# A transformer program's opening: the second slab's split ahead of the root, rotations at one lag, parameter transposes two units earlier

## The chip, the cores and the metric

One core of one Trainium2 chip. The metric is the device time in microseconds of one execution of the whole program; lower is better.

## The reference, cut to what matters

Two blocks of a network on 256 rows of width 1024, float32. The change lies in the first steps of the first block:

```
n = rms_norm(x, ln_mix_g)
proj = n @ w_in                      # 1024 x 5888
qa, ka, va, ... = split(proj)        # 768 columns each for q, k, v of the dilated attention
qa = rope(qa);  ka = rope(ka)        # 12 heads of 64: x*cos + rot(x)*sin
```

After it come a dilated and a stick-breaking attention, gates, a cross attention with a memory, a convolutional gated MLP, and a second block of two layers, whose last part is a mixture of 8 experts.

## The kernel before, in words

Every float32 product is made of three matmuls on parts: a number is split into a high part (ScalarE copies it to the rounded type) and a residual (VectorE subtracts). The weights come as slabs of 1 MB, transferred on SyncE's queue in the order of a plan into five raw buffers. A slab is split (`begin_split`, line 381: ScalarE's copy at L394 at once, VectorE's residual at L398 when the returned function is called) into one of three split buffers. Slab n goes into buffer n modulo 3, so its split waits until the products of slab n - 3 have released that buffer (`over`), and for the slab's landing. The raw buffer that a residual frees is given to the next transfer (`send`). `W.take` hands slab n to the products and first queues the splits of all slabs up to n + 2 (n + 1 in its first call).

Each engine works through its own queue in the order in which the program appends to it; waits are on semaphores that count an engine's operations.

The opening: x is transposed (`turn_rows`) and split; slab 0 is split in two halves (`split_half`). The squares of x are summed on ScalarE in four pieces (`square_half`, L630); `root_of` (L639 to L511) makes the inverse root from them on VectorE in small steps; `diagonal` (L648) makes two diagonal matrices of it, and `over_columns` (L657, L660) spreads them into R1, with which cosine and sine are multiplied (L786). The normalisation of q and k is thus applied in the rotation.

Then 12 units of 128 columns are made, two to a slab: units 0 to 5 are q, 6 to 11 are k. A unit is 24 matmuls (`wstat`; L438 to L440) into one PSUM bank. `rotate(unit)` multiplies the unit with sine (L769) and with cosine (L770) on VectorE; the second frees the bank. If another rotation is pending, `rope_finish` closes the older one: a pair of matmul records with the matrix `rot` on TensorE (L745) into a new bank, and an add on VectorE (L748). `ps.take()` gives the 8 banks in turn (0 to 7, and round again); each unit, each `rope_finish`, `over_columns` and `other_params` take one.

`other_params` transposes the staged parameters with four matmuls (L709) and copies them to `prm` on ScalarE (L712). They are needed from the memory's rows on. The squares of the memory (`sq2`) are made in the steps of units 5 and 7. Behind unit 11 come the two slabs of v (`v_proj`, "va"); the rotations still open are made after the first of them.

The order of takes up to the loop, from the code: `turn_rows` for k = 0, 1 take banks 0 and 1, the first parameters' transpose 2, `turn_rows` for k = 2 to 7 take 3 to 7 and 0, units 0 and 1 take 1 and 2. In the loop of before: unit 2, `over_columns`, unit 3, unit 4, and from there on finishing pairs and units as the code has them.

Of the kernel before, what the change touches and what calls it, by code (L numbers as in the profile page):

```python
# [154 lines left out]
def program(nc, x, mem, consts, w, out, cap):  # L155
    ctx = ExitStack()
    with ctx:
# [296 lines left out]
        def wstat(W_, o, nH, nL, m, kcs, start, stop, *waits, by=None):  # L454

            H, L, ready, _ = W_

            def product(e, q, a, b):
                return mm3(e, o, H[:, a, m * 128:(m + 1) * 128], L[:, a, m * 128:(m + 1) * 128],
                           nH[:, b, :], nL[:, b, :], start and q == 0, stop and q == len(kcs) - 1)  # L460
            return chunks_of(product, kcs, by, ready, *waits)
# [37 lines left out]
        def newton(cols, t):  # L499


            guess = 1597463007.0 - 2.0 ** 30 - 2.0 ** 22

            def both(make):
                for tb in range(len(cols)):
                    t[tb] = dve.op(make(*cols[tb]), t[tb])
            both(lambda y, d, u: lambda e: e.tensor_scalar(y.bitcast(I32), d.bitcast(I32), -0.5, guess,
                                                           ALU.mult, ALU.add))
            for _ in range(3):
                both(lambda y, d, u: lambda e: e.scalar_tensor_tensor(u, y, y, d, ALU.mult, ALU.mult))  # L510
                both(lambda y, d, u: lambda e: e.scalar_tensor_tensor(y, u, 1.5, y, ALU.add, ALU.mult))  # L511
            return t
# [14 lines left out]
        def stat(q, slot, tb):  # L527
            return sm[:, 32 * q + slot + tb:32 * q + slot + tb + 1]
# [84 lines left out]
        def cload(t, first, last, eng=None):  # L613

            c0, c1_ = CCOL[first][0], sum(CCOL[last])
            return [load(t[:, 0:c1_ - c0], consts[:, c0:c1_], eng=eng)]
# [3 lines left out]
        W = Weights(lambda: lc1.extend(cload(c1, "rot", "sin", sp)))  # L620
# [8 lines left out]
        def square_half(src, junk, slot, tb, h, *waits):  # L629
            return act.op(lambda e: e.activation(  # L630
                junk[:, tb, 512 * h:512 * h + 512], src[:, tb, 512 * h:512 * h + 512], ACT.Square,
                accum_out=stat(3 + h, slot, tb)), *waits)

        def root_of(slot, last):

            t = []
            for tb in range(2):
                c0 = stat(3, slot, tb)
                t.append(dve.op(lambda e, c0=c0: e.tensor_scalar(c0, c0, -0.5 / 1024, -0.5 * EPS, ALU.mult, ALU.add),  # L639
                                last[tb, 0]))  # L640
            for tb in range(2):
                c0, c1_, d = (stat(q, slot, tb) for q in (3, 4, 5))
                t[tb] = dve.op(lambda e, c0=c0, c1_=c1_, d=d: e.scalar_tensor_tensor(
                    d, c1_, -0.5 / 1024, c0, ALU.mult, ALU.add), t[tb], last[tb, 1])
            return sm[:, slot:slot + 2], newton([[stat(q, slot, tb) for q in (0, 5, 6)] for tb in range(2)], t)

        def diagonal(D, r, tr):
            return [dve.op(lambda e, tb=tb: e.tensor_scalar(D[:, tb, :], ident, r[:, tb:tb + 1], None, ALU.mult),  # L648
                           tr[tb]) for tb in range(2)]

        def over_columns(R, D, td, *waits):

            b = ps.take()

            def f(e):
                for tb in range(2):
                    last = e.matmul(banks[b][:, 128 * tb:128 * tb + 128], ones, D[:, tb, :], start=True, stop=True)  # L657
                return last
            t = pe.op(f, td, lc, ps.free[b])
            tR = act.op(lambda e: e.activation(R[:, :], banks[b][:, 0:256], ACT.Copy), t, *waits)  # L660
            ps.free[b] = [tR]
            return tR
# [11 lines left out]
        def split_rows(bt, gname, H, L, k):  # L674
            b, t = bt
            g = split_from_psum(H[:, k, :], L[:, k, :], banks[b][:, 0:256], t, tprm, scale=pcol(gname, k))
            ps.free[b] = g
            return g
# [17 lines left out]
        W.split_half(0)  # L696
        nx += [split_rows(turned[k], "ln_mix_g", nAH, nAL, k) for k in range(4, 8)]
        W.split_half(1)
        sq1[1, 1] = square_half(X, scr, 0, 1, 1, lx[1])
        rx, trx = root_of(0, sq1)  # L700
        tdx = diagonal(D1, rx, trx)
        mem_cols, mem_row = [], []

        def other_params():
            b = ps.take()

            def f(e):
                for i in range(4):
                    last = e.transpose(banks[b][:, i * 128:(i + 1) * 128], stage[:, i, :], ident)  # L709
                return last  # L710
            t = pe.op(f, rest, ps.free[b])
            tp = act.op(lambda e: e.activation(prm[:, 16:512], banks[b][:, 16:512], ACT.Copy), t)  # L712
            ps.free[b] = [tp]
# [28 lines left out]
        def rope_finish():  # L742
            unit, i, tsin, tcos = rope_pending.pop(0)
            b = ps.take()
            t = pe.op(lambda e: e.matmul(banks[b][:, 0:256], rot, rsc[i], start=True, stop=True),  # L745
                      tsin, ps.free[b], lc1)
            dst = (qA if unit < 6 else kA)[:, unit % 6, :]
            t2 = dve.op(lambda e: e.tensor_tensor(dst, banks[b][:, 0:256], rcs[i], ALU.add), t, tcos)  # L748
            rfree[i] = [t, t2]
            ps.free[b] = [t2]  # L750
            qk_ready[unit] = t2
# [11 lines left out]
        def rotate(unit):  # L763

            b, t = made.pop(unit)
            i = rope_n[0] % 2
            rope_n[0] += 1
            wt = [t, trig, rfree[i]]
            t1 = dve.op(lambda e, b=b, i=i: e.tensor_tensor(rsc[i], banks[b][:, 0:256], sinT, ALU.mult), *wt)  # L769
            t2 = dve.op(lambda e, b=b, i=i: e.tensor_tensor(rcs[i], banks[b][:, 0:256], cosT, ALU.mult), *wt)  # L770
            ps.free[b] = [t2]
            rope_pending.append((unit, i, t1, t2))
            if len(rope_pending) > 1:
                rope_finish()

        for unit in range(2, 12):
            if unit % 2 == 0:
                Wt = W.take("qk")
            b = ps.take()
            t = wstat(Wt, banks[b][:, 0:256], nAH, nAL, unit % 2, all8, True, True, ps.free[b], by=nx)  # L780
            if unit % 2:
                W.release(Wt[3], t)
            made[unit] = (b, t)
            if unit == 2:
                tRx = over_columns(R1, D1, tdx)
                trig = [dve.op(lambda e, c=c: e.tensor_tensor(c, c, R1[:, :], ALU.mult), tRx, lc1)  # L786
                        for c in (sinT, cosT)]
            else:
                rotate(unit - 3 + (unit > 4))
                if unit == 4:  # L790
                    rotate(2)
            if unit in (5, 7):
                for h in range(2):
                    sq2[unit // 7, h] = square_half(M, junkM, 2, unit // 7, h, lm)
            if unit == 9:
                other_params()

        def v_proj(key, ncols, dst, nH, nL, ndy):

            bb = [ps.take(), ps.take()]  # L800
            for s in range(2):
                Wt = W.take(key)
                for tb in range(2):
                    t = tstat(Wt, banks[bb[tb]][:, 0:ncols], nH, nL, tb, [(k, 4 * s + k) for k in range(4)],
                              (0, ncols), s == 0, s == 1, ndy, ps.free[bb[tb]] if s == 0 else None)
                    if s == 1:
                        ps.free[bb[tb]] = [dst(tb, banks[bb[tb]][:, 0:ncols], t)]
                W.release(Wt[3], t)
                yield
# [3 lines left out]
        def put(dstf, toks, r, tr):  # L813
            def g(tb, src, t):
                toks.append(act.op(lambda e: e.activation(dstf(tb), src, ACT.Copy, scale=r[:, tb:tb + 1]), t, tr[tb]))
                return toks[-1]
            return g

        nm = []
        for s, _ in enumerate(v_proj("va", 512, put(lambda tb: vA[:, tb, 0:512], va_t, rx, trx), nAH, nAL, nx)):  # L820
            if s == 0:
                for unit in (10, 11):
                    rotate(unit)
                rope_finish()

# [1653 lines left out]
```

How the kernel before makes its waits and increments, by code:

```python
    def wait(self, *waits):  # L90
        need = {}
        for w in flat(waits):
            sem, v = w
            if need.get(sem.name, (None, 0))[1] < v:
                need[sem.name] = w
        for name, (sem, v) in need.items():
            if self.seen.get(name, 0) < v:
                self.seen[name] = v
                self.items.append(lambda e, sem=sem, v=v: e.wait_ge(sem, v))
# [1 line left out]
    def op(self, fn, *waits, inc=True):  # L101
        self.wait(*waits)
        if inc:
            self.n += 1
            self.items.append(lambda e: fn(e).then_inc(self.sem, 1))
        else:
            self.items.append(fn)
        return (self.sem, self.n)
# [95 lines left out]
        def load(dst, src, *waits, eng=None):  # L205
# [1 line left out]
            small_at[0] += 1  # L207
            q = eng or act
            before = (c.sem, c.n)
            t = c.next()
            q.wait(before if before[1] else None, *waits)
            q.items.append(lambda e: e.dma_start(dst, src).then_inc(c.sem, 16))
            return t
# [2190 lines left out]
            def f(e):  # L2404
                with e.If(overflow[q] > 0):
                    for item in inner:
                        item(e)
                with e.Else():
                    if n1 > n0:
                        e.wait_ge(q.sem, n0)
                        e.sem_inc(q.sem, n1 - n0)
                    for count, inc in dmas.items():
                        if count.n > inc:
                            e.wait_ge(count.sem, count.n - inc)
                        e.sem_inc(count.sem, inc)
```

## Time and profile before

| | |
|---|---|
| median of 3 runs | 1889.77 us (1889.28 to 1893.27) |
| the profiled execution | 1892.46 us |
| its span, first to last instruction | 1890.6 us |
| TensorE busy | 97% of the span |
| VectorE, ScalarE busy | 79%, 62% |
| mean granted TensorE clock | 0.993 of full speed |

Times in rows are microseconds from the start of the span. Engines: PE is TensorE, PEld its weight loads, DVE is VectorE, ACT ScalarE, SPq the transfers that SyncE issues. A row of the timeline gives start, duration, engine, line, operation, output and inputs, count, and in brackets the engine's idle time just before and what ended it. Two neighbouring rows may overlap a little, since instructions are pipelined.

### The profile page before, as it was taken

What the parts mean: (1) busy time and instruction counts of PE and PEld (TensorE: products, weight loads), DVE (VectorE), ACT (ScalarE), POOL (GpSimd) and SP (SyncE); (2) the same over time, 40 slices, a digit from 0 to 9 for tenths busy, and PEclk for the clock granted to TensorE, in tenths of its full rate; (3) what the DMA queues carried; (4) which work ended last, traced back from release to release, by engine and by line L of the source; (5) the groups of instructions that cost most, each with busy time, mean ns of one, the idle gap of its engine ahead of it and who ended that gap; (6) DMA issues with size and microseconds to landing.
All of it is one profiled execution on the core that took longest, in us unless ns stands there. A gap on an engine that the chain in (4) does not pass through costs nothing.

```text
span 1890.6 us, 25921 instructions
## 1 busy us (share of the span) xinstructions
PE 1835.4 (97%) x10249; PEld 1594.7 (84%) x10249; DVE 1487.2 (79%) x1633; ACT 1166.1 (62%) x1103; POOL 56.6 (3%) x71
## 2 busy tenths in 40 slices
PE   7999998999999999998999999999999999999997
PEld 7888978899888999996888888888888888888885
DVE  6664667776796655696888889989898898998897
ACT  4445656555553443443777777777777777777775
POOL 0000000000320000230000000000000000000000
PEclk9999999999999999999999999999999999999998
DMA  9434433755461756454799999999999999999993
GB/s 323 139 106 134 157 112 112 244 187 185 132 195 58 227 200 201 124 195 161 269 373 372 361 349 372 360 371 357 350 365 361 375 369 342 365 366 366 371 359 122
DMA packets 258047, 495.70 MB, mean 262 GB/s; under 512 B 9625, under 2 KB 99455, under 8 KB 257919
## 3 DMA queue, kind: packets, MB, share of 16 engines
q1 hardware_dynamic: 253263, 489.04, 73.5%
q10 hardware_dynamic: 4656, 4.93, 0.9%
q8 instruction: 84, 1.38, 0.3%
q14 instruction: 44, 0.36, 0.1%
HBM read 492.89 MB, written 1.05 MB: 261 GB/s over the span
## 4 chain that ended last, share of the span: by engine, by line
PE 89%; DVE 6%; ACT 4%; issue 1%; DMA 0%; DVEq 0%; SPq 0%; ACTq 0%
PE bank L438 27%; PE bank L440 27%; PE bank L439 27%; DVE splitL L398 2%; PE bank L1798 2%; ACT splitH L394 2%; PE bank L2191 1%; PE bank L2122 1%; PE bank L1905 1%; PE bank L1200 0%; PE bank L2161 0%; PE bank L2160 0%; PE bank L899 0%; ACT RAH L480 0%; PE bank L956 0%
## 5 line engine op out<-in xcount | busy, mean ns | idle before, releaser
L398 DVE TENSOR_TENSOR splitL<-raw,splitH 128x2048 fp32r<-128x2048 f32 (+1 forms) x338 | 768.8, 2278 | 170.6 <-ACT splitH L394 163.1
L394 ACT ACTIVATE splitH<-raw 128x2048 fp32r<-128x2048 f32 (+1 forms) x338 | 641.2, 1902 | 151.0 <-PE bank L440 132.8
L438 PE MATMUL bank<-splitH,RBH 128*128 128x512 f32 x960 | 380.9, 397 | 3.4 <-DVE splitL L398 2.4
L440 PE MATMUL bank<-splitH,RBL 128*128 128x512 f32 x960 | 375.1, 391 | 0.0
L439 PE MATMUL bank<-splitL,RBH 128*128 128x512 f32 x960 | 374.7, 390 | 0.0
L438 PE MATMUL bank<-RAH,splitH 128*128 128x256 f32 x1088 | 311.4, 286 | 7.7 <-DVE RAL L484 3.8
L439 PE MATMUL bank<-RAL,splitH 128*128 128x256 f32 x1088 | 307.7, 283 | 0.0
L440 PE MATMUL bank<-RAH,splitL 128*128 128x256 f32 x1088 | 307.7, 283 | 0.0
L438 PEld LDWEIGHTS bank<-RAH,splitH 128*128 128x128 f32 x1088 | 208.4, 192 | 12.0 <-ACT RAH L480 6.6
L438 PEld LDWEIGHTS bank<-splitH,RBH 128*128 128x128 f32 x960 | 180.7, 188 | 40.8 <-ACT splitH L394 2.3
L440 PEld LDWEIGHTS bank<-splitH,RBL 128*128 128x128 f32 x960 | 180.5, 188 | 38.7
L398 DVE TENSOR_TENSOR splitL<-rawx,splitH 128x2048 fp32r<-128x2048 f32 x84 | 192.4, 2291 | 25.4 <-ACT splitH L394 24.1
L439 PEld LDWEIGHTS bank<-splitL,RBH 128*128 128x128 f32 x960 | 181.0, 189 | 35.5
L439 PEld LDWEIGHTS bank<-RAL,splitH 128*128 128x128 f32 x1088 | 208.5, 192 | 1.0
L440 PEld LDWEIGHTS bank<-RAH,splitL 128*128 128x128 f32 x1088 | 208.5, 192 | 0.0
L394 ACT ACTIVATE splitH<-rawx 128x2048 fp32r<-128x2048 f32 x84 | 161.1, 1918 | 46.4 <-PE bank L440 46.4
L438 PE MATMUL bank<-splitH,hTH 128*128 128x512 f32 x448 | 174.5, 390 | 0.0
L439 PE MATMUL bank<-splitL,hTH 128*128 128x512 f32 x448 | 174.4, 389 | 0.0
L440 PE MATMUL bank<-splitH,hTL 128*128 128x512 f32 x448 | 174.3, 389 | 0.0
L398 DVE TENSOR_TENSOR splitL<-rawx_scr,splitH 128x2048 fp32r<-128x2048 f32 x41 | 94.0, 2292 | 11.2 <-ACT splitH L394 10.2
L440 PEld LDWEIGHTS bank<-splitH,hTL 128*128 128x128 f32 x448 | 84.1, 188 | 17.6
L438 PEld LDWEIGHTS bank<-splitH,hTH 128*128 128x128 f32 x448 | 84.1, 188 | 17.1
(324 smaller groups left out, 2245.8 us busy)
## 6 DMA issues: line engine op xcount, KB each, us to landing
raw<-in_moe_wg SPq DMA_DIRECT2D x71, 1024.0 KB, 6.7
raw<-in_moe_wu SPq DMA_DIRECT2D x71, 1024.0 KB, 6.9
raw<-in_moe_wd SPq DMA_DIRECT2D x69, 1024.0 KB, 6.9
rawx<-in_moe_wd SPq DMA_DIRECT2D x29, 1024.0 KB, 7.0
rawx<-in_moe_wu SPq DMA_DIRECT2D x28, 1024.0 KB, 6.8
rawx<-in_moe_wg SPq DMA_DIRECT2D x27, 1024.0 KB, 6.9
raw<-in_w_in SPq DMA_DIRECT2D x24, 1024.0 KB, 6.7
raw<-in_w_up SPq DMA_DIRECT2D x22, 1024.0 KB, 5.1
```

Source lines behind the costliest of these rows:

```text
L394: a = act.op(lambda e: e.activation(h[:, 0:size], r[:, 0:size], ACT.Copy), self.landed[n], over)
L398: d = dve.op(lambda e: e.tensor_tensor(l[:, 0:size], r[:, 0:size], h[:, 0:size].bitcast(F), ALU.subtract), self.landed[n], over, a)
L438: e.matmul(o, lh, rh, start=start, stop=False)
L439: e.matmul(o, lh, rl, start=False, stop=False)
L440: return e.matmul(o, ll, rh, start=False, stop=stop)
L1798: last = e.matmul(banks[b][:, 0:256], diag[:, k, :], hc[:, 0, 2 + k:258 + k], start=(k == 0), stop=(k == 30))
L1905: last = e.matmul(banks[b][:, 0:256], pww[:, k, 128 * u:128 * u + 128], sq[:, k, :], start=(k == 0), stop=(k == 2))
L2122: last = e.matmul(banks[b][:, 256 * c:256 * c + w_], src[:, tb, d:d + 128], Pm[:, tb, 0:w_], start=(tb == 0), stop=(tb == 1))
L2191: last = e.transpose(banks[b][:, 128 * k:128 * k + 128], hh[q % 2][:, 128 * k:128 * k + 128], ident)
```

## The change

Four edits: ScalarE's part of slab 1's split is queued ahead of the last piece of the squares, and its residual ahead of the root; `rotate` is called once in each step from unit 3 on, for the unit three before (before: from unit 5 on for the unit two before, with two calls in the step of unit 4); `other_params` is called in the step of unit 7 instead of 9; the rotation of unit 9 thereby falls behind the first slab of v. The call of `W.take("qk", 1)` further down finds slab 1 split already.

```
         W.split_half(1)
+        rest_of_second = W.begin_split()
         sq1[1, 1] = square_half(X, scr, 0, 1, 1, lx[1])
+        rest_of_second()
         rx, trx = root_of(0, sq1)
         tdx = diagonal(D1, rx, trx)
-        mem_cols, mem_row = [], []
...
             else:
-                rotate(unit - 3 + (unit > 4))
-                if unit == 4:
-                    rotate(2)
+                rotate(unit - 3)
             if unit in (5, 7):
                 for h in range(2):
                     sq2[unit // 7, h] = square_half(M, junkM, 2, unit // 7, h, lm)
-            if unit == 9:
+            if unit == 7:
                 other_params()
...
             if s == 0:
-                for unit in (10, 11):
+                for unit in (9, 10, 11):
                     rotate(unit)
                 rope_finish()
```

## Rows read from the trace of the kernel before

**Rows 1.** The page: busy times by engine, and the chain that ended last.

```profile
PE 1835.4 (97%) x10249; PEld 1594.7 (84%) x10249; DVE 1487.2 (79%) x1633; ACT 1166.1 (62%) x1103; POOL 56.6 (3%) x71
...
PE 89%; DVE 6%; ACT 4%; issue 1%; DMA 0%; DVEq 0%; SPq 0%; ACTq 0%
```

**Rows 2.** Windows: length, busy times with instruction counts, granted clock, DMA share, GB/s.

```profile
26.00:31.00 5.00, 3.49 (x27) 3.06 (x25) 3.13 (x4) 3.08 (x5) 0.00 (x0) 1.00 1.03 407
...
76.00:110.00 34.00, 34.00 (x259) 31.36 (x260) 21.11 (x32) 14.90 (x20) 0.00 (x0) 1.00 0.29 94
```

**Rows 3.** Timeline of TensorE, 17 to 62 us.

```profile
17.77 0.28 PE L440 MATMUL bank<-RAH,splitL 128*128 128x256 f32 x1
19.30 0.35 PE L438 MATMUL bank<-RAH,splitH 128*128 128x256 f32 x1 [1.25 <-DVE splitL L398]
...
28.45 0.60 PE L745 MATMUL bank<-SC,c 128*128 128x256 f32 x2
30.55 0.70 PE L745 MATMUL bank<-SC,c 128*128 128x256 f32 x2 [1.51 <-DVE SC L769]
...
37.26 0.60 PE L745 MATMUL bank<-SC,c 128*128 128x256 f32 x2
...
40.56 0.60 PE L745 MATMUL bank<-SC,c 128*128 128x256 f32 x2
...
47.59 0.60 PE L709 MATMUL bank<-cb,stage 128*128 128x128 f32 x4
...
50.91 0.60 PE L745 MATMUL bank<-SC,c 128*128 128x256 f32 x2
...
60.11 1.02 PE L745 MATMUL bank<-SC,c 128*128 128x256 f32 x4
61.67 0.70 PE L745 MATMUL bank<-SC,c 128*128 128x256 f32 x2 [0.54 <-DVE SC L769]
```

**Rows 4.** Timeline of VectorE, 14 to 61 us.

```profile
14.53 0.21 DVE L639 TENSOR_SCALAR sm<-sm 128x1 f32<-128x1 f32 x2
...
16.87 4.49 DVE L398 TENSOR_TENSOR splitL<-raw,splitH 128x2048 fp32r<-128x2048 f32 x2
...
27.87 2.29 DVE L398 TENSOR_TENSOR splitL<-raw,splitH 128x2048 fp32r<-128x2048 f32 x1 [2.58 <-ACT splitH L394]
30.08 0.42 DVE L769 TENSOR_TENSOR SC<-bank,c 128x256 f32<-128x256 f32 x1
...
38.44 0.42 DVE L769 TENSOR_TENSOR SC<-bank,c 128x256 f32<-128x256 f32 x1
38.78 0.42 DVE L770 TENSOR_TENSOR SC<-bank,c 128x256 f32<-128x256 f32 x1
...
39.56 0.42 DVE L769 TENSOR_TENSOR SC<-bank,c 128x256 f32<-128x256 f32 x1
...
60.74 0.42 DVE L748 TENSOR_TENSOR kA<-bank,SC 128x256 f32<-128x256 f32 x1 [1.29 <-PE bank L745]
```

**Rows 5.** Timeline of ScalarE, 12 to 49 us.

```profile
12.90 0.68 ACT L630 ACTIVATE scr<-X 128x512 f32<-128x512 f32 x1
...
13.51 1.96 ACT L394 ACTIVATE splitH<-raw 128x2048 fp32r<-128x2048 f32 x1
...
34.22 1.92 ACT L394 ACTIVATE splitH<-raw 128x2048 fp32r<-128x2048 f32 x1 [4.50 <-DMA raw<-in_w_in]
...
40.82 1.92 ACT L394 ACTIVATE splitH<-raw 128x2048 fp32r<-128x2048 f32 x1 [3.46 <-PE bank L440]
48.23 0.59 ACT L712 ACTIVATE prm<-bank 128x496 f32<-128x496 f32 x1 [5.50 <-PE bank L709]
48.71 1.91 ACT L394 ACTIVATE splitH<-raw 128x2048 fp32r<-128x2048 f32 x1
```

**Rows 6.** The transfer of slab 5: issue, and time from issue to landing.

```profile
L350 SPq DMA_DIRECT2D raw<-in_w_in x1: 372/372/372, 24.5 to 24.5; - x1
...
DMA to landing us min/median/max: 9.7/9.7/9.7
```

**Rows 7.** Windows near 495 us, columns as in rows 2.

```profile
491.00:494.00 3.00, 1.05 (x5) 0.58 (x5) 2.82 (x2) 3.00 (x3) 0.00 (x0) 1.00 0.00 0
...
495.10:498.60 3.50, 3.50 (x10) 2.68 (x10) 3.50 (x4) 0.09 (x1) 0.00 (x0) 0.54 1.09 302
```

More of the change, by code:

```diff
@@ L698, in program @@
         W.split_half(1)
+        rest_of_second = W.begin_split()
         sq1[1, 1] = square_half(X, scr, 0, 1, 1, lx[1])
+        rest_of_second()
         rx, trx = root_of(0, sq1)
         tdx = diagonal(D1, rx, trx)
-        mem_cols, mem_row = [], []
         def other_params():
@@ L788, in program @@
             else:
-                rotate(unit - 3 + (unit > 4))
-                if unit == 4:
-                    rotate(2)
+                rotate(unit - 3)
             if unit in (5, 7):
@@ L794, in program @@
                     sq2[unit // 7, h] = square_half(M, junkM, 2, unit // 7, h, lm)
-            if unit == 9:
+            if unit == 7:
                 other_params()
@@ L821, in program @@
             if s == 0:
-                for unit in (10, 11):
+                for unit in (9, 10, 11):
                     rotate(unit)
```

## The prediction

> **What bounds the kernel now.** The page first: TensorE is busy for 97% of the span and the chain of work that ended last is 89% TensorE [rows 1]. So what TensorE loses in the opening is lost at the end, unless a later stage waits for something else. The windows answer that: from 76 to 110 us TensorE is busy all the time and the DMA engines 0.29 [rows 2]; transfers are started by splits, these follow the products, and the whole shifts as one. The question is when TensorE starts the product after the last rotation of q and k.
>
> The timeline of TensorE over the opening shows where it stops [rows 3]. At 19.30 it waited for slab 1's residual (its last product before would have handed over at 17.77 + 0.12 = 17.89): 1.41 us. At 30.55 it waited for the sine product of unit 1: the finishing pair of unit 0 started at 28.45, the next could have at 28.88: 1.67 us. At 61.67 the pair of unit 11 waited: 0.5 us. In between nothing is missing; one unit and one pair take 3.30 us (37.26 to 40.56). I write F4 for the finishing matmul pair of unit 4 (L745), S4 and C4 for its sine and cosine products (L769, L770), P for the parameter transposes (L709).
>
> **Offsets, all from rows.** A pair that waits for a VectorE product starts 0.47 after that product starts (30.08 to 30.55). Cosine follows sine by 0.34, and the next unit's sine by 1.12 [rows 4]. A residual holds the sine behind it for 2.21 (27.87 to 30.08). From the start of ScalarE's part of a split to the sine behind its residual: 4.22 (34.22 to 38.44) [rows 4, 5]; so 2.01 to the residual. A split whose buffer is released by a unit starts 0.26 after the pair behind it (40.56 to 40.82). P to ScalarE's copy 0.64, from there to the split behind it 0.48, P to the next pair 3.32 [rows 3, 5].
>
> **Slab 1 first.** ScalarE's part moves from 13.51 to 12.90, the start of the squares that it passes; there was no wait for the landing at 13.51, and if there is one up to then the result is the same within 0.1. Residual at 14.91; before, product followed the residual's start by 2.43 (16.87 to 19.30), so it could start at 17.34 and does at 17.89: 1.41 gained. What is pushed back: the root takes 2.34 on VectorE (14.53 to 16.87), now from 17.12, its diagonals are ready near 19.5 and TensorE asks for them behind unit 2, near 20.8. Residuals 2 and 3 slip by about 0.4 and 0.2; they are wanted after 24 and 30 us. They cost nothing behind these products; were the cover gone, 0.4. Slab 6's transfer waits in SyncE's queue for residual 1, but SyncE comes to it only after 24.5, when the parameter loads are issued [rows 6]: no transfer starts earlier for the move.
>
> **One rotation per step.** Nothing stands between F0 (28.45 - 1.41 = 27.04) and unit 5; F1 comes one unit later, at 30.34. Split 4 also moves 1.41 earlier, S1 to 28.67, so F1 doesn't wait: the 1.67 are gained too. F2 at 33.64, F3 would be at 36.94.
>
> **What is late next.** S3 now stands where S4 stood, behind residual 5, and slab 5 doesn't come earlier: issued at 24.5, 9.7 us to landing, 34.2 [rows 6], and ScalarE's idle time before 34.22 is put down to this transfer. Its place in SyncE's queue is untouched, and the DMA engines are full (share 1.03 in 26 to 31) [rows 2]. So S3 and C3 stay at 38.44 and 38.78.
>
> Then the accumulator banks. They are taken in turn, one a unit and one a pair, eight in all. Counted through from the first transposes (unit 3 takes 5, unit 4 6, F0 7): unit 5 bank 0, F1 1, unit 6 2, F2 3, unit 7 4, F3 5, P 6, unit 8 7, F4 0, unit 9 1, F5 2, unit 10 3, F6 4. So F3 takes unit 3's bank and waits for C3, P waits for C4, F4 for C5, F6 for C7. C5 and C7 are queued behind the residual of the very same step. Before, with units rotated one step earlier, a pair's bank had been free for a step; the trace of before has no such wait, so its price is bounded by nothing below and by these sums above, and I take the sums since the semaphores leave no choice.
>
> F3: C3 38.78 + 0.47 = 39.25 (2.31 late). P: C4 38.78 + 1.12 + 0.47 = 40.37, where 39.68 would do (0.69). P is now ahead of split 6 on ScalarE: split 6 starts at 40.37 + 0.64 + 0.48 = 41.49, though its buffer was released near 37. F4: C5 is at 41.49 + 4.22 + 0.34 = 46.05, F4 at 46.52, where 40.37 + 3.32 = 43.69 would do: 2.83 lost. F5 3.30 later, 49.82 (C6 is done). Split 7 is at 50.08, C7 at 54.64, F6 at 55.11, where 53.12 would do: 1.99. Before, the pair in this place (F7) was at 50.91: 4.20 later. Next comes F7 with no wait, since P's bank is long free.
>
> **The end.** With T the start of the first pair after the first value product (60.11 before): add at T + 0.63 (60.74), next sine 0.45 later, pair 0.47 after that: 61.67 as seen. Now four pairs, with two rotations still to be made behind an add: one more step of 1.12. So 4.20 + 1.12 = 5.3 late at the product that follows. A pair after a stall takes some 0.1 longer to hand over, an estimate from 0.70 against 0.60 for L745 [rows 3], twice: 5.3 to 5.5. In the stalls' terms: gained 1.41, 1.67, 0.43 (one pair fewer up to F6) and the 0.1 that the restart after 30.55 cost; lost 2.31 + 0.69 + 2.83 + 1.99 = 7.82; that makes the 4.20, and 1.12 at the end.
>
> The profiled execution took 1892.46 for a span of 1890.6; its sum would be 1897.9. The median of the three is 1889.77, 2.7 lower, and the shift is the same: 1889.8 + 5.4 = **1895.2 us**.
>
> **Rivals.** First, the clock. After a stretch with TensorE busy 1.05 of 3 us (491 to 494) the granted clock fell to 0.54 over 495.1 to 498.6 [rows 7], the lower level, 1.2 GHz, for most of it, which costs 0.46 x 3.5 = 1.6. My forecast has two such stretches. After the first (busy some 0.4 in 37.2 to 40.4) the slow product of unit 8 would end by 45.4, before F4 at 46.52: hidden. After the second it would fall on unit 9 and cost 1.6: 1896.8. For it: 2.5 us idle in one piece; against: 1.51 us idle before 30.55 was followed by no fall. The Trainium skill, "TensorE: Matmul & The Clock Gate", section "Why this matters for your kernels", warns that idle gaps between bursts of matmuls send the clock to half rate; rows 7 agree. 0.14.
>
> Second, not slower: the banks don't bind, because the order in which they come round is other than I count, or the owner is released earlier. Then F3 is at 38.44 + 0.47 = 38.91, P 39.34, F4 42.66, F6 49.26, 1.65 ahead of 50.91; minus the end's 1.12: 0.5 faster, 1889.2. It decides if C5 is not asked for by F4. Against it: the count. 0.12.
>
> Third, the change does just what it says, and slab 5 has room too: F3 at 36.94, F6 at 47.3, 3.6 ahead, minus 1.12: 2.5 faster, 1887.3. Landing at 34.2 speaks against it. 0.06. Even this is within 0.2%.
>
> Fourth, part is given back: the clock falls that exist later (one is shown [rows 7]) are met at another time, and one less is 1.6 less: 3.8 slower, 1893.6. 0.10.
>
> **How the numbers follow.** The forecast has 0.58, the four rivals 0.14, 0.12, 0.06, 0.10. The forecast's own range is 1893.8 to 1897.0: a slab 5 landing half a microsecond off moves all by as much, and the runs of before are 4 us apart. With the clock's and the fourth: 1891.5 to 1898.0; it leaves out the second and third, 0.18. A measurement here can tell about 0.2%, 3.8 us: slower the forecast nearly always, the clock rival, and half of the fourth: 0.70; within: the second and third, the other half, and a low draw: 0.27; faster 0.03.
>
> **What would show it.** After: no idle time before unit 2's product; F1 without a wait; L745 pairs that wait for VectorE's L770 at about 39.2, 46.5 and 55.1; L709 near 40.4 and ScalarE's split behind it near 41.5; four pairs before the second value slab, the last near 67. Wrong if F4 starts at the end of unit 8 (the count of banks), if slab 5 lands well before 34, or if what follows 68 us comes less than 3.5 us later than before.

## The result, and the profile after

| | before | changed |
|---|---|---|
| median | 1889.92 us (9 runs) | 1900.28 us (1896.04 to 1901.37, 9 runs) |
| ratio | | 1.0043 (1.0035 to 1.0051) |
| the profiled execution | 1892.46 us | 1897.79 us, span 1896.0 |

The changed kernel is slower, as forecast, and by more: 1895.2 was predicted, 1898.0 was the upper end. Run again beside the experiments on two further occasions it was at 1.0027 (1.0015 to 1.0039) and 1.0035 (1.0021 to 1.0048). One of the twelve executions of the kernel with banks apart (below) took 2620.72 us at a mean granted clock of 0.654, and its ratio leaves that one out.

First TensorE's timeline of the changed kernel, the counterpart of [rows 3]. The finishing pairs (F) are now at L746, cosine products at L771, the transposes P at L710.

```profile
28.23 0.60 PE L746 MATMUL bank<-SC,c 128*128 128x256 f32 x2
...
31.53 0.60 PE L746 MATMUL bank<-SC,c 128*128 128x256 f32 x2
...
39.75 0.70 PE L746 MATMUL bank<-SC,c 128*128 128x256 f32 x2 [1.46 <-DVE SC L771]
...
40.96 0.63 PE L710 MATMUL bank<-cb,stage 128*128 128x128 f32 x4 [0.51 <-DVE SC L771]
...
47.13 0.70 PE L746 MATMUL bank<-SC,c 128*128 128x256 f32 x2 [2.67 <-DVE SC L771]
...
50.53 0.60 PE L746 MATMUL bank<-SC,c 128*128 128x256 f32 x2
...
55.83 0.96 PE L746 MATMUL bank<-SC,c 128*128 128x256 f32 x2 [1.83 <-DVE SC L771]
...
60.75 0.60 PE L746 MATMUL bank<-SC,c 128*128 128x256 f32 x2
...
66.66 1.02 PE L746 MATMUL bank<-SC,c 128*128 128x256 f32 x4
68.56 1.49 PE L746 MATMUL bank<-SC,c 128*128 128x256 f32 x4 [0.88 <-DVE SC L771]
69.69 0.58 PE L438 MATMUL bank<-splitH,RAH 128*128 128x512 f32 x1
```

These are F0, F1, F3, P, F4, F5, F6, F7, then F8 to F11, and the product behind them. The two waits of [rows 3] at 19.30 and 30.55 are gone. Before the end three pairs and the transposes wait instead, and what they wait for is not the sine product that they read but the cosine product L771, whose result they don't read: it frees the bank into which they write. The 0.88 ahead of F10, at 68.56, is of the same kind: counted on from F6, F10 gets the bank of unit 10. That one costs nothing, as is shown below under "The end".

The chain of work that ended last, over the same stretch, shows the mechanism up to F4 in one column (start, duration, what):

```profile
24.87 9.82 DMA raw<-in_w_in
...
34.71 1.93 ACT splitH L394
...
36.74 2.29 DVE splitL L398
39.03 0.33 DVE SC L770
39.37 0.33 DVE SC L771
39.70 0.34 DVE qA L749
...
40.06 0.42 DVE SC L770
40.48 0.34 DVE SC L771
...
40.96 0.64 PE bank L710 x4
...
41.63 0.59 ACT prm L713
42.21 1.81 ACT splitH L394
...
44.11 2.29 DVE splitL L398
46.41 0.34 DVE SC L770
46.74 0.34 DVE SC L771
...
47.13 0.70 PE bank L746 x2
```

Read upwards from 47.13: F4 waits for unit 5's cosine, that stands behind slab 6's residual, that behind ScalarE's half of the split, that behind the copy of the parameters, that behind P, P behind unit 4's cosine, and that behind slab 5's residual and landing. TensorE's own products of units 7 and 8 are not in it: in the kernel before they were the chain here.

**Where the times part.** The product behind the last pair starts at 69.69; before, it followed the pair at 61.67 [rows 3] at 62.02. That is 7.7 us, of which 5.4 are left at the end of the span. Two marks in both traces (first and last start of a group; the first two rows are of the kernel before, the others of the changed one) show where about 2 us come back:

```profile
L1781 PE MATMUL bank<-vn,wsT x32: 275/275/351, 547.3 to 837.5; 128*128 128x96 f32 x32
L1536 ACT ACTIVATE fb<-up x22: 418/418/420, 612.9 to 774.3; 128x256 f32<-128x256 f32 x22
```

```profile
L1780 PE MATMUL bank<-vn,wsT x32: 275/275/351, 554.9 to 843.3; 128*128 128x96 f32 x32
L1535 ACT ACTIVATE fb<-up x22: 417/418/418, 618.7 to 780.1; 128x256 f32<-128x256 f32 x22
```

7.6 late at 547, 5.8 late at 613. In between the granted clock of the kernel before was low once (553 to 557), that of the changed one never. So the profiled execution flatters the change: it is 2.5 us below the median of the changed kernel, that of before 2.5 above its own. And the changed kernel's opening holds a low stretch of its own behind F6. Windows, columns as in rows 2, the first of the kernel before, the others of the changed one:

```profile
12.00:15.00 3.00, 2.94 (x24) 2.98 (x25) 3.00 (x11) 3.00 (x5) 0.00 (x0) 1.00 1.08 356
```

```profile
12.00:15.00 3.00, 3.00 (x14) 3.00 (x15) 2.65 (x6) 3.00 (x3) 0.00 (x0) 1.00 1.07 355
...
53.50:57.00 3.50, 1.67 (x9) 1.34 (x8) 2.45 (x4) 0.00 (x0) 0.00 (x0) 0.88 0.19 26
57.00:60.40 3.40, 3.40 (x21) 3.40 (x21) 1.00 (x3) 0.00 (x0) 0.00 (x0) 0.63 0.83 281
```

The last row is unit 11's product, right behind the wait of F6: F6 to F7 takes 4.92 where 3.30 to 3.41 is the step at full clock. The first two rows, 24 matmuls against 14 in the same 3 us, are taken up in the last section.

### The profile page after: what moved, and what is told of

Same layout as the page of the kernel before. It is cut to its first block, busy times and chain, and to the rows that moved or that the text cites. A ratio compares the mean times of both kernels' runs of the same rounds, so it can differ in the third digit from the quotient of the medians.

```text
span 1896.0 us, 25921 instructions
## 1 busy us (share of the span) xinstructions
PE 1835.8 (97%) x10249; PEld 1594.9 (84%) x10249; DVE 1487.1 (78%) x1633; ACT 1165.6 (61%) x1103; POOL 56.4 (3%) x71
## 4 chain that ended last, share of the span: by engine, by line
PE 87%; DVE 6%; ACT 4%; SPq 1%; issue 1%; DMA 1%; DVEq 0%; ACTq 0%
PE bank L438 27%; PE bank L440 26%; PE bank L439 26%; DVE splitL L398 3%; ACT splitH L394 2%; PE bank L1797 1%; PE bank L2190 1%; PE bank L2121 1%; SPq L212 1%; PE bank L1904 1%; DMA raw<-in_w_in 1%; SPq L350 0%; PE bank L1199 0%; PE bank L2159 0%; PE bank L2160 0%
```

## The experiments

All were timed beside the kernel before. "P" and "F" as above; the start of the product behind the last pair (62.02 before, 69.69 changed) is the mark by which the traces are compared.

**The first edit alone.**

```
         W.split_half(1)
+        rest_of_second = W.begin_split()
         sq1[1, 1] = square_half(X, scr, 0, 1, 1, lx[1])
+        rest_of_second()
```

> The kernel before with the first edit alone: slab 1's split ahead of the last squares and of the root. Theory (the edit does what it says, nothing behind it is held by another thing): unit 2's product starts at about 17.9 instead of 19.3, the pair of unit 1 still waits 1.5 us for its sine, unit 4's pair may just wait for the sine behind slab 5, 0.1 or less; 1.3 to 1.4 us stay at 68 us and at the end, 1888.5, ratio 0.9993. Rival (all that is gained is taken back by slab 5's landing near 34.2): 1889.9, ratio 1.0000.

1890.76 us, ratio 0.9994 (0.9986 to 1.0003). The profile: F0 at 28.12, F1 at 30.23 after a wait of 1.51, mark 61.70. Unit 2's product doesn't wait, but only 0.3 us are left. The products of units 0 and 1 ran at the lower clock for a while in this execution, as in the changed kernel's (15 matmuls in 12 to 15 us; 24 in the kernel before), and that took 1.3 us back before F0: it comes 16.20 us after the first product of unit 0, and 14.90 in the next run. Both theories lie in the interval, so this run can't tell between them, and no other run here has the first edit with the rotations as they were.

**Banks apart.** The pairs take two banks of their own.

```
+        pair_ring = Banks(banks)
+        pair_ring.use([7, 2])
         def rope_finish():
...
-            b = ps.take()
+            b = pair_ring.take()
...
+        ps.use([3, 4, 5, 6, 0, 1])
         for unit in range(2, 12):
...
+        ps.use([5, 6, 7, 0, 1, 2, 3, 4])
         def turn_memory(ks):
```

> The changed kernel, but the finishing pairs take banks 7 and 2 in turn and the units the other six, so no pair shares a bank with a unit that is still to be rotated. Theory (bank waits cost the time): no pair waits for a cosine product (L771); the pair of unit 3 waits for its sine alone, near 39.4; those of units 4 and 6 don't wait; the product after the last pair starts near 62.2 instead of 69.7 (before: 62.0), in all 1890.0, ratio 1.000. Rival (slab 5's landing and the rotation at lag three are the cause, with banks a mark in the trace only): as the changed kernel, 1896 to 1900.

1891.0 us, ratio 0.9994 (0.9985 to 1.0003), where the changed kernel is at 1.0027 to 1.0043. This is the run that decides. Timeline of TensorE; pairs are at L749, the sine product at L773, cosine at L774:

```profile
38.80 0.70 PE L749 MATMUL bank<-SC,c 128*128 128x256 f32 x2 [2.07 <-DVE SC L773]
...
44.59 0.60 PE L749 MATMUL bank<-SC,c 128*128 128x256 f32 x2
...
61.95 0.70 PE L749 MATMUL bank<-SC,c 128*128 128x256 f32 x2 [0.54 <-DVE SC L773]
63.08 0.70 PE L749 MATMUL bank<-SC,c 128*128 128x256 f32 x2 [0.42 <-DVE SC L773]
63.42 0.58 PE L438 MATMUL bank<-splitH,RAH 128*128 128x512 f32 x1
```

F4 (44.59) and F6 have no wait left. F3 still waits, and longer than in the changed kernel, though TensorE came to it 1.6 us earlier (its clock was up from the start here): slab 5 holds it. What releases it now is the sine product, its own operand. So what TensorE gains ahead of F3, the first edit's share with it, is taken by slab 5. The mark is 1.4 later than before; unit 8's product took 4.45 (40.14 to 44.59) instead of 2.95, a clock fall behind F3's wait (granted clock 0.60 over 40.0 to 43.5), and at full clock it would be level.

**Parameters in the step of unit 5.**

```
-            if unit == 7:
+            if unit == 5:
                 other_params()
```

> The changed kernel with the parameter transposes in the step of unit 5. ScalarE's copy of them is then no longer ahead of slab 6's split; the bank order keeps the same kind of conflict, with the pair of unit 3 now on unit 4's bank. Theory: that pair at about 40.9 (1.1 later than 39.75), slab 6's split near 38.5 instead of 42.1, the pair of unit 4 near 45.0 instead of 47.13, that of unit 6 near 53.7 instead of 55.8: 2 us less than the changed kernel in a run with as many clock falls, 1894 to 1898. Rival (the place of the parameters costs nothing): as the changed kernel.

1899.17 us, ratio 1.0037 (1.0024 to 1.0050): no gain. The expectation had counted the banks one short:

```profile
39.20 0.43 PE L438 MATMUL bank<-RAH,splitH 128*128 128x256 f32 x1 [3.20 <-DVE SC L771]
...
48.96 0.70 PE L746 MATMUL bank<-SC,c 128*128 128x256 f32 x2 [1.83 <-DVE SC L771]
...
59.15 0.39 PE L438 MATMUL bank<-RAH,splitH 128*128 128x256 f32 x1 [1.39 <-DVE SC L771]
```

With P a step earlier, unit 7's product itself gets unit 3's bank, and unit 11's that of unit 7 (59.15). When a pair waits, the product of its step is done already; here the product waits 3.20 us first and is then still to be done, and slab 6's split, released by it, comes later too (43.93, in the changed kernel 42.11). The mark is 71.06; the profiled execution is the slowest of the five (1904.46), and its clock fell behind the waits of 3.20 and 1.83. That P's place costs nothing is not shown by it either; the copy is tried by itself below.

**The waits filled.** Transposes of a constant into a free bank, ahead of F3, F4 and F6.

```
+        fill = {3: (6, 3), 4: (11, 5), 6: (7, 2)}
...
+            if unit in fill:
+                n, spare = fill[unit]
+                def g(e):
+                    for _ in range(n):
+                        last = e.transpose(banks[spare][:, 0:128], ones, ident)
+                    return last
+                pe.op(g, ps.free[spare])
```

> The changed kernel with idle TensorE work ahead of the three pairs that wait (6, 11 and 7 transposes of a constant into a bank that is free): same waits, but TensorE isn't idle in them. Theory (what the runs show above the profiled one's 6 us is the lower clock that follows the waits): no fall of the granted clock before 70 us, the waits end as in the changed kernel, times near 1896 in nearly all runs, a mean clock of 0.993 or more. Rival (the clock has no part): times spread as in the changed kernel, 1896 to 1901, median 1900.

1895.59 us, 1893.83 to 1899.20, ratio 1.0022 (1.0012 to 1.0032), mean clock 0.993 to 0.995 in all eight runs. The three waits end about when they did (within 0.5), F4 at 46.77, F6 at 55.47:

```profile
43.94 1.36 PE L753 MATMUL bank<-cb 128*128 128x128 f32 x11
46.77 0.70 PE L756 MATMUL bank<-SC,c 128*128 128x256 f32 x2 [1.47 <-DVE SC L781]
```

The clock doesn't fall behind them, F6 to F7 is 3.40, the mark is at 67.81. It was low at 13.1, ahead of all waits, which the expectation had ruled out. The fill ahead of F3 waited itself, for the add that freed its bank, and covers little.

**Filled once more, and the changed kernel beside it.**

> The kernel with the waits filled once more, in one call with the changed kernel. Theory (clock falls behind the three waits cost 1 to 3 us a run): its median is 2 to 4 us below the changed kernel's, few runs at a mean clock under 0.993. Rival (the falls are moved, not avoided, or cost nothing): medians within 1 us.

> The changed kernel in the same call: 5 to 8 us above the kernel before; its runs at a mean clock of 0.991 or 0.992 are 3 us or more above those at 0.994.

Filled: 1895.69 us, 1.0023 (1.0015 to 1.0032), mark 67.95. Changed: 1898.82 us, 1.0035 (1.0021 to 1.0048), mark 70.43. The medians are 3.1 us apart, the intervals overlap. The filled kernel has four of twelve runs at 0.991 or 0.992, more than "few". The changed kernel's runs at 0.990 to 0.992 took 1899.1 to 1900.9, its two at 0.994 1895.8 and 1897.6. So 7.6 us above the kernel before as expected, and the means of the two groups are 3.5 us apart. The windows of its profile:

```profile
44.00:47.00 3.00, 0.62 (x3) 0.56 (x4) 2.33 (x3) 0.00 (x0) 0.00 (x0) 0.99 1.06 327
47.00:50.00 3.00, 3.00 (x16) 3.00 (x15) 1.18 (x3) 0.00 (x0) 0.00 (x0) 0.50 1.02 324
...
57.00:61.00 4.00, 4.00 (x22) 3.98 (x21) 1.18 (x3) 0.00 (x0) 0.00 (x0) 0.57 0.84 261
```

F4 to F5 takes 4.91 and F6 to F7 4.90: two falls of 1.5 us each, one behind each long wait. The filled kernel's own profile has none before 70 us and yet is one of its slowest executions (1899.84), so what makes an execution slow lies in part further on.

**The changed kernel on the second occasion.**

> The changed kernel itself once more, beside the others on the same chip. Theory: 0.4% above the kernel before; the waits at the pairs of units 3, 4 and 6 as before to 0.5 us; where the clock falls behind them differs from run to run, and the runs with a mean clock of 0.991 are the slow ones. Rival (the difference was one of chips): within 0.2%.

1898.06 us, 1.0027 (1.0015 to 1.0039), between the two expectations; mark 70.34. Waits at F3 0.60, P 0.51, F4 2.67, F6 1.83. The clock falls at 47.1 and at 57.3. Its six runs have 0.992 to 0.994 and don't order by it: 0.991 doesn't occur.

**The copy behind the split.** `other_params` returns its ScalarE copy as a function, called in the step of unit 8 behind `W.take`.

```
+            def copy():
+                tp = act.op(lambda e: e.activation(prm[:, 16:512], banks[b][:, 16:512], ACT.Copy), t)
+                ps.free[b] = [tp]
+            return copy
...
                 Wt = W.take("qk")
+            if unit == 8:
+                copy_params()
```

> The changed kernel with ScalarE's copy of the parameters queued behind its part of slab 6's split instead of ahead of it. Theory: that part starts near 38.4 instead of 42.1, the residual near 41.2, the pair of unit 4 doesn't wait (44.3 instead of 47.1), that of unit 6 still does; 2.8 us less than the changed kernel, and fewer clock falls. Rival (the bank alone costs it): the pair of unit 4 still waits over 2 us.

1896.89 us, 1.0025 (1.0014 to 1.0036), mark 66.70, 3.0 earlier than the changed kernel's. Of the 2.8 us expected in the time, 1.2 are seen against the changed kernel beside it (1898.06), which the intervals can't tell; the trace decides. First ScalarE, then TensorE:

```profile
38.67 1.91 ACT L394 ACTIVATE splitH<-raw 128x2048 fp32r<-128x2048 f32 x1 [0.86 <-PE bank L440]
41.58 0.59 ACT L715 ACTIVATE prm<-bank 128x496 f32<-128x496 f32 x1 [1.01 <-PE bank L710]
```

```profile
44.26 0.60 PE L749 MATMUL bank<-SC,c 128*128 128x256 f32 x2
...
52.85 0.79 PE L749 MATMUL bank<-SC,c 128*128 128x256 f32 x2 [1.83 <-DVE SC L774]
```

F4's wait of 2.67 is gone with the bank order unchanged, F6's 1.83 stands. So the largest wait needed both: the shared bank (banks apart takes it away too), and the copy ahead of the split in ScalarE's queue.

**Slab 5 first on SyncE's queue.** The parameter, memory and mask loads are queued behind its transfer.

```
-        rest = param_loads(PARAMS[2:], 16, sp)
-        lm = load(M[:, :, :], mr, eng=sp)
-        lmask = cload(c1[:, 768:2304], "maskA", "maskB", sp)
...
         W.split_half(1)
+        rest = param_loads(PARAMS[2:], 16, sp)
+        lm = load(M[:, :, :], mr, eng=sp)
+        lmask = cload(c1[:, 768:2304], "maskA", "maskB", sp)
```

> The changed kernel with the small parameter loads, the memory and the masks queued on SyncE behind slab 5's transfer, which then is issued near 14.7 instead of 24.9. Theory (slab 5's landing makes the first two waits, the banks the others): it lands near 26; ScalarE's part of slab 5's split follows unit 5 near 31.8 instead of 34.7, the pair of unit 3 and the transposes don't wait, that of unit 4 still waits for its cosine product, near 44.7 instead of 47.1; 2.4 us less than the changed kernel. Rival (the landing is hidden): no change against it.

1899.83 us, 1.0039 (1.0026 to 1.0052). The trace has half of what was expected, the time none that can be told. ScalarE:

```profile
31.39 0.63 ACT L627 ACTIVATE junkM<-M 128x512 f32<-128x512 f32 x1 [5.22 <-DMA M<-in_mem]
...
32.63 1.90 ACT L394 ACTIVATE splitH<-raw 128x2048 fp32r<-128x2048 f32 x1
```

The split is 2.1 us earlier (34.71), and is now held by the squares of the memory ahead of it in ScalarE's queue, whose transfer the move has delayed. F3 at 37.65 still waits 0.72, F4 at 45.02 2.66, mark 67.56.

**Catch-up.** Banks apart, and two rotations in the step of unit 9.

```
-                rotate(unit - 3)
+                rotate(unit - 3 - (unit > 9) + 2 * (unit > 9))
+                if unit == 9:
+                    rotate(7)
...
-                for unit in (9, 10, 11):
+                for unit in (10, 11):
```

> The kernel with banks apart, and in the step of unit 9 two rotations (6 and 7), so that the lag is two from there on and only units 10 and 11 stay for the end. Theory: no wait from the pair of unit 4 to unit 11; at the end one step of 1.1 us less than with banks apart, the last pair waits 0.5 us as in the kernel before; 1.1 us less than with banks apart (ratio 0.9994): 0.9988 to the kernel before. Rival (two rotations in one step make the second pair wait, as in the kernel before at unit 4): a wait of 0.5 to 1.5 us there, ratio as with banks apart.

> Banks apart and catch-up once more, beside the version with slab 5's transfer ahead: 0.9983 to the kernel before, if the first result was no matter of its chip; the version with the transfer ahead is 1 to 2 us below it.

1888.01 us, 0.9983 (0.9974 to 0.9992), and again 1888.68 us, 0.9985 (0.9977 to 0.9994): faster than both kernels, by 0.15 to 0.17% against the kernel before. Marks 61.18 and 61.35. The four records at 46.32 are F5 and F6, with no wait; the last pair waits as in [rows 3]. The third row is of the second of the two profiles: F3 waited 2.07 us there, as with banks apart, and this time no fall followed (granted clock 1.00 up to 62 us).

```profile
46.32 1.03 PE L749 MATMUL bank<-SC,c 128*128 128x256 f32 x4
...
60.83 0.70 PE L749 MATMUL bank<-SC,c 128*128 128x256 f32 x2 [0.54 <-DVE SC L773]
```

```profile
38.90 0.70 PE L749 MATMUL bank<-SC,c 128*128 128x256 f32 x2 [2.07 <-DVE SC L773]
```

Catch-up in the one common ring of banks was not run, nor was the kernel before with banks apart, so how the gain divides among the edits isn't shown.

**Catch-up with slab 5 first,** now in the order slab 5, memory, parameters, masks.

> Banks apart, catch-up in the step of unit 9, and SyncE's queue in the order slab 5, memory, parameters, masks. Theory (slab 5's landing is what is left of the waits before the end): ScalarE's part of slab 5's split follows unit 5 at once, no pair waits before the last, the product after the last pair starts 1 to 2 us earlier than 61.2; ratio 0.9975 to the kernel before. Rival (later slabs or the memory's landing take its place): 0.9983 as with catch-up alone.

1888.05 us, 0.9981 (0.9971 to 0.9990). The split starts at 31.73, behind unit 5's product. Nothing waits up to the last pair:

```profile
38.07 0.60 PE L749 MATMUL bank<-SC,c 128*128 128x256 f32 x2
...
59.62 0.70 PE L749 MATMUL bank<-SC,c 128*128 128x256 f32 x2 [0.54 <-DVE SC L773]
59.97 0.58 PE L438 MATMUL bank<-splitH,RAH 128*128 128x512 f32 x1
```

The mark is 1.2 to 1.4 us earlier than with catch-up alone, as the theory has it; the medians, 0.6 us apart beside each other, can't tell.

## Why the prediction was right or wrong

**Slab 1 first.** Right: residual at 14.80 (14.91), product without a wait. The 1.41 us hung on a clock that the profiled opening of before had and the changed kernel's had not: F0 at 28.23 instead of 27.04. Up to F3 that makes no difference, since slab 5 takes up whichever slack there is: with banks apart F0 is at 26.67 and F3 at 38.80, in the catch-up kernel they are at 28.27 and 38.71.

**The lag of three** removed the wait of 1.67 as forecast.

**Slab 5's landing.** Right: ScalarE's half at 34.71 (34.2), F3 held. Slab 5 first removes it.

**The banks.** Right, to each wait. F3 39.75 (39.25), P 40.96 (40.37), F4 47.13 (46.52), F6 55.83 (55.11): late by 0.5 to 0.7, nearly all from the 0.5 by which ScalarE's half of slab 5's split was late (34.71 for 34.22). In the other two profiles of the changed kernel it was not late (33.91 and 33.97), and F4 is at 46.32 and 46.38, 0.1 to 0.2 early. Banks apart takes the waits for cosine products away, the copy behind the split takes F4's alone. The rival "the banks don't bind" falls, and with F3 held in every profile of the changed kernel the rival by which slab 5 has room falls too.

**The end.** Right. F8 (the prediction's T) to the mark is 3.03, as with T + 2.67 and 0.35. The prediction's count of banks stops at F6 and so misses F10's wait for unit 10's cosine; it moves nothing, since with banks apart, without that wait, F8 to the mark is 3.03 as well (60.39 to 63.42).

**The clock: here it failed.** The step that failed is the clock term. The forecast's sum has it at nothing, and the only fall that the prediction allows is a rival with 0.14, one of 1.6 us, behind F4. The third wait, F6's 1.99, was not looked at, though it is longer than the 1.51 that the prediction has as followed by no fall. In three profiles of the changed kernel the clock fell behind F6 each time (56.1, 57.3, 57.2) and behind F4 twice (47.1, 46.9), 1.5 us each; in the two filled ones behind neither. With the term in it the sum comes out: 5.4, the 0.6 that slab 5 was late and one fall make 7.5 for the first profile, 5.4 and two falls make 8.4 for the other two; the marks say 7.7, 8.3 and 8.4.

From the mark to the median more is open. 8.4 on 1889.8 is 1898.2, just above the range; the medians are 10.4, 6.1 and 7.6 apart on the three occasions. The 5.4 is near the size at full clock: the lowest runs of the two kernels are 6.8, 6.1 and 6.1 apart, and the filled kernel, with marks 5.8 and 5.9 late, is 4.0 and 4.5 above the kernel before. What a wait costs TensorE is its length and, in some executions, 1.5 us more in the unit behind it. How much of the medians' difference is the opening's falls, and how much other falls met differently later, is not settled, nor are the 2 us that the first occasion has beyond two falls; the fill's 3 us is in overlapping intervals.

**From the profile to the median.** The prediction took the shift to be the same for both. The profiled execution came out at 1897.79 where its sum says 1897.9, and that is luck: the mark was 2.2 to 2.4 later than in the sum, and about as much was given back behind it. The median, 10.4 higher, had no such luck.

**The rival that part is given back** describes the profiled execution (2 us back near 553), not the median.

## What to carry to other kernels

When work on one engine is made to lag, count the buffers in the order in which they are handed round: a longer lag keeps a bank one step longer, and the wait appears at whoever takes it next, with a releaser that it never reads. Separate rings for the short-lived and the long-lived cost nothing that the traces show (no unit waits for a bank in them), took the change from 1.0027 to 1.0043 back to 0.9994, and together with catching up before the end made it a small gain. Each wait of TensorE should be priced by itself with the clock fall that may follow it (1.5 us here), not all together by one.

## What the runs showed of the hardware

The granted clock in the windows is 1.00 for 12 to 15 us in the changed kernel, but 14 matmuls start there and 24 in the kernel before. The steps from one matmul to the next say why: 0.21 us (12.46 to 12.67) against 0.12 in the kernel before, and 0.21 is also the step at 57 us, where the column reads 0.50. So TensorE was at the lower of its levels, 1.2 GHz against 2.4 GHz, in a stretch where the column doesn't tell it. Nine of the fourteen profiles had a slow stretch there (14 to 19 matmuls; in seven of them the column says 1.00) and five had not (24 to 27), with the same matmuls to do. Matmul counts per microsecond, not the clock column, tell it in an opening.

The granted clock fell behind every wait of 1.83 us at F6 that was not filled: in all three profiles of the changed kernel, with the copy behind the split and with slab 5 first. It fell behind F4's 2.66 to 2.67 us in two of the four profiles that have that wait, and behind F3's 2.07 us in one of two. So the length of the wait alone doesn't decide, and one program meets a different number of falls from execution to execution. The Trainium skill, "TensorE: Matmul & The Clock Gate", section "Why this matters for your kernels", warns of idle gaps between bursts of matmuls; these runs agree that a fall can follow one, but the gaps here were shorter than those that it names (1.83 us at F6).
